# A fourth slot for expert weights, x1 read back for the last stage, and another order of the weight loads

## The reference

```
g_sel = argmax(x1 @ w_rg + b_rg)                 # 1 of 4 groups
top 2 of the 4 experts of that group             # weights from softmax, renormalised
h_e = silu(x1 @ w_gate[e]) * (x1 @ w_up[e])      # 1024 -> 256, 16 experts in all
y   = sum over a token's two experts of weight * (h_e @ w_down[e])
out = LN2(alpha * x1 + y)
```

## Time and profile before

| | us |
|---|---|
| median of 3 runs | 827.02 (824.53, 827.02, 830.73) |
| the profiled execution | 824.47 |
| its span, first to last instruction | 822.5 |
| TensorE busy | 740.1 (90%) |
| VectorE busy | 555.3 (68%) |
| ScalarE busy | 391.7 (48%) |
| GpSimd busy | 43.7 (5%) |
| DMA moved | 129.86 MB, mean 158 GB/s |

### The profile page before, as it was taken

How to read it: one execution, slowest core, us unless ns; L and a number is a source line. 1 busy time by engine, 2 the same in 40 slices (tenths; PEclk the granted TensorE clock), 3 DMA queues, 4 the chain that set the end, 5 groups by cost and what they waited for, 6 DMA issues and landing times.

```text
span 822.5 us, 13533 instructions
## 1 busy us (share of the span) xinstructions
PE 740.1 (90%) x5359; PEld 648.1 (79%) x5359; DVE 555.3 (68%) x1020; ACT 391.7 (48%) x651; POOL 43.7 (5%) x39
## 2 busy tenths in 40 slices
PE   6999999999999999888899999998459988899784
PEld 5989999999998999666678999998447766676531
DVE  4244966888644877998753565755648888888537
ACT  4348752558327332344555432111237877778502
POOL 0000000000000000000000000000010111010064
PEclk8999999999999999999999999999569999999977
DMA  7333122221333241332101963812427999999263
GB/s 235 103 112 101 52 70 86 66 68 26 122 108 116 66 148 53 116 129 69 67 29 42 351 232 107 299 45 83 160 77 255 378 389 386 385 387 386 68 230 115
DMA packets 92799, 129.86 MB, mean 158 GB/s; under 512 B 8576, under 2 KB 75136, under 8 KB 92736
## 3 DMA queue, kind: packets, MB, share of 16 engines
q1 hardware_dynamic: 87072, 112.21, 40.2%
q0 software_dynamic: 3360, 12.06, 4.2%
q10 hardware_dynamic: 2304, 4.72, 1.5%
HBM read 109.02 MB, written 19.81 MB: 157 GB/s over the span
## 4 chain that ended last, share of the span: by engine, by line
PE 67%; DVE 14%; issue 7%; ACT 6%; DMA 5%; SPq 1%; POOL 0%; ACTq 0%; DVEq 0%; POOLq 0%
PE pp L813 25%; PE pw L1134 12%; PE pp L1011 5%; PE pp L1157 5%; PE pp L793 3%; PE pw L871 2%; ACT w_hi L1226 2%; DVE w_lo L1672 2%; PE pp L1120 2%; DVE Lm L1861 1%; PE pw L980 1%; PE pw L1198 1%; DMA xtok<-in_x_sample_dram 1%; PE pp L769 1%; PE pw L1033 1%
## 5 line engine op out<-in xcount | busy, mean ns | idle before, releaser
L813 PE MATMUL pp<-x_hi,w_hi 128*128 128x288 f32 (+1 forms) x608 | 187.8, 309 | 2.6 <-DVE w_lo L1672 1.2
L813 PE MATMUL pp<-x_lo,w_hi 128*128 128x288 f32 (+1 forms) x608 | 179.6, 295 | 0.0
L813 PE MATMUL pp<-x_hi,w_lo 128*128 128x288 f32 (+1 forms) x608 | 179.4, 295 | 0.0
L813 PEld LDWEIGHTS pp<-x_hi,w_hi 128*128 128x128 f32 (+1 forms) x608 | 114.9, 189 | 10.6 <-issue 7.6
L813 PEld LDWEIGHTS pp<-x_lo,w_hi 128*128 128x128 f32 (+1 forms) x608 | 113.9, 187 | 0.2
L813 PEld LDWEIGHTS pp<-x_hi,w_lo 128*128 128x128 f32 (+1 forms) x608 | 113.7, 187 | 0.0
L1672 DVE TENSOR_TENSOR w_lo<-w_raw,w_hi 128x2048 fp32r<-128x2048 f32 (+1 forms) x30 | 67.1, 2236 | 43.7 <-ACT w_hi L1226 43.5
L2103 DVE TENSOR_TENSOR glo<-wgu,ghi 128x1024 fp32r<-128x1024 f32 x64 | 76.6, 1219 | 19.0 <-ACT ghi L1502 18.8
L1502 ACT ACTIVATE ghi<-wgu 128x1024 fp32r<-128x1024 f32 x64 | 65.7, 1052 | 22.4 <-DMA wgu<-in_w_up_dram 22.4
L1134 PE MATMUL pw<-ghi,xTh 128*112 128x512 f32 x128 | 53.2, 416 | 14.7 <-issue 12.3
L1226 ACT ACTIVATE w_hi<-w_raw 128x2048 fp32r<-128x2048 f32 (+1 forms) x30 | 56.0, 1865 | 5.7 <-ACT gring L1262 4.1
(11 more groups left out here) (327 smaller groups left out, 1662.2 us busy)
## 6 DMA issues: line engine op xcount, KB each, us to landing
w_raw<-in_w_in_dram SPq DMA_DIRECT2D x23, 1024.0 KB, 5.5
wgu<-in_w_gate_dram SPq DMA_DIRECT2D x16, 1024.0 KB, 11.3
wgu<-in_w_up_dram SPq DMA_DIRECT2D x16, 1024.0 KB, 14.5
wd<-in_w_down_dram SPq DMA_DIRECT2D x16, 1024.0 KB, 9.0
ys_d<-ysb SPq DMA_DIRECT2D x16, 448.0 KB, 11.2
gates_d<-gring ACTq DMA_DIRECT2D x16, 288.0 KB, 2.1
w_raw<-in_w_out_dram SPq DMA_DIRECT2D x4, 1024.0 KB, 6.5
gates_early<-gates_d SPq DMA_DIRECT2D x4, 576.0 KB, 4.0
```

The lines of the kernel that those rows point to most:

```text
L813: mm = pe.matmul(pp[0:wide, b, 0:HT], lw, rx, start=(k == 0 and y == 0), stop=(k == last and y == 2))
```

## The change

WS becomes 4. The fourth gate-and-up slot lies at `mixer_end`, on `xr` tiles 0 to 3, and the fourth down slot 16 KB further, on tile 4 of `xr` and on row 0 of `lnr`, which the second norm does not read. So expert 3's weights are loaded as soon as all of x1 is stored and turned, and expert 4's are the first that wait for a slot. x1 is read back from `x1_d` into `xr` at the end: tiles 0 to 3 after the last gate and up, tile 4 after the last down, and the scaling by alpha stands behind that. In SP's loop, the load of down for e-1 comes after the loads of gate and up for e and waits for down of e-5; the store in that turn is that of e-6 and comes last.

```diff
-WS = 3
+WS = 4
...
-        gate_up_at = (spare, raw_start, spare + 16384)
-        down_at = (o_start, raw_start + 16384, raw_start + 24576)
+        gate_up_at = (spare, raw_start, spare + 16384, mixer_end)
+        down_at = (o_start, raw_start + 16384, raw_start + 24576, mixer_end + 16384)
...
-        s_xr = sem("s_xr")
+        s_xr, s_xr4 = sem("s_xr"), sem("s_xr4")
...
             expert_gate_up(2)
             store_x1(NT - 1)
             expert_down(2)
+            sp.wait_ge(s_x1d, 16 * NT)
+            sp.wait_ge(s_tx, 2 * NT)
+            expert_gate_up(3)
+            expert_down(3)
...
             for e in range(WS, NX):
                 sp.wait_ge(m_gu, e - WS + 1)
                 expert_gate_up(e)
-                if e >= WS + 1:
-                    store_y(e - WS - 1)
-                sp.wait_ge(m_y, e - WS + 1)
-                expert_down(e)
-            for e in range(NX - WS - 1, NX):
+                if e > WS:
+                    sp.wait_ge(m_y, e - WS)
+                    expert_down(e - 1)
+                if e >= WS + 2:
+                    store_y(e - WS - 2)
+            sp.wait_ge(m_y, NX - WS)
+            expert_down(NX - 1)
+            for e in range(NX - WS - 2, NX - 2):
                 store_y(e)
+            sp.wait_ge(m_gu, NX)
+            sp.dma_start(xr[:, 0:4, :], x1_d[0:TP].rearrange("(i p) d -> p i d", p=P)).then_inc(s_xr, 16)
+            store_y(NX - 2)
+            store_y(NX - 1)
+            sp.wait_ge(m_y, NX)
+            sp.dma_start(xr[0:64, 4, :], x1_d[TP:T]).then_inc(s_xr4, 16)
...
-                if e < NT:
-                    if e == 0:
-                        dve.wait_ge(s_x1d, 16 * NT)
-                    dve.tensor_scalar(xr[:, e, :], xr[:, e, :], ALPHA, None, ALU.mult).then_inc(s_dg, 1)
             for f in range(2):
                 down_low(NX - 1, f)
             hidden_low(NX - 1)
+            for i in range(NT):
+                r = ROWS[i]
+                if i < 4:
+                    dve.wait_ge(s_xr, 112)
+                else:
+                    dve.wait_ge(s_xr4, 16)
+                dve.tensor_scalar(xr[0:r, i, :], xr[0:r, i, :], ALPHA, None, ALU.mult).then_inc(s_dg, 1)
...
                 if i == 0:
+                    dve.wait_ge(s_dg, NT)
                     dve.wait_ge(s_yg[0], 32)
```

## The result

The changed kernel takes 829.44 us (median of 20 runs, 827.15 to 837.33) against 827.25 us for the kernel before (20 runs, 823.67 to 830.73): a ratio of 1.0032, 95% interval 1.0016 to 1.0048. By the ratio that is 2.6 us more, by the medians 2.2. A second series gave 1.0021 [1.0001, 1.0041]. The forecast was 825.5 us, a gain of 1.5: the sign was wrong. The median still lies inside the stated range, 816.5 to 830, but outside the forecast's own part of it, 822 to 828.5.

What follows compares the result with a forecast made beforehand. DMA was taken to bound the expert stage: a loss of 7.7 to 10.1 us in place of 10.4, tail 0, gain taken as 1.5 us, giving 825.5 us from the median 827.02; range 816.5 to 830.

Steps and rivals of the forecast that it cites:

- the forecast's own part: Whole kernel: 0.3 to 2.7 us gained, 822 to 828.5 us with the runs' spread, chance 0.62.
- the saturated turn: SP's queue in the expert stage: with engines saturated, one expert's loads and store take 10.5 us per turn.
- the tail: After the last experts: x1 reload and scaling delay the residuals 1.3 us, hidden under the gathered-rows wait; net 0.
- The fifth tile's load: Tail: 256 KB of x1 read back after the last store, taking about 3 us alone.
- rival B: Tail reload makes results 6.2 us late, 831.7 us; sign: PE waits over 5 us for scaling; chance 0.09.
- A: Expert stage: only weights were awaited, stores hold nobody up; all experts run at 9.5 us, 816.6 us; chance 0.17.
- the price of the turn that holds y(0): SP's queue, turn of e=6: takes 12.6 us as before, y(0) lands at 647.7, in time by 1.3 us.
- the 7.7 forecast: Expert stage: y(9), the last store behind loads, lands at 742.2, needed at 734.5, 7.7 us late.
- a slow first turn: SP's queue: if the first turn stays at 12.9 us for 10.5, y(9) is 10.1 us late.
- The loss of 10.4 us: Expert stage before: gu(5) to gu(15) took 114.9 us where the free pace of 9.5 us needs 104.5.
- Rival C: Expert stage: slow first turn and slightly longer turns give back the early weights' lead; 827 to 829 us, chance 0.12.

Runs made afterwards that it cites:

- the second trace: Profile from repeating the changed kernel unedited, an execution of 830.23 us; that series measured 828.17 us, 1.0021 of the kernel before.
- the first trace: First profile of the changed kernel, an execution of 834.53 us; the median of its 20 runs was 829.44 us.
- experiment 6: Changed kernel with the store of y(e-5) in place of y(e-6) in the turn of e, and a third result buffer: 813.48 us, 0.9824 of the kernel before.
- experiment 4: Changed kernel with a third result buffer, queue order untouched: 819.88 us, 0.9909 of the kernel before.
- experiment 5: Kernel before, three slots and old queue order, with only x1 read back and scaled at the end: 826.55 us, 0.9988.
- experiment 2: Changed kernel with the old queue order, store of y(e-5) ahead of the down load, four slots and reload kept: 824.44 us, 0.9971 of the kernel before.
- experiment 9: Changed kernel with the store of y(e-6) moved in front of the down load of its turn: 828.04 us, 1.0017 of the kernel before.

## Why the prediction was wrong

**What held.** The mechanism: DMA bound before; expert 3's weights loaded in the idle stretch with no cost that a row shows; the result copy waiting for y(k) up to y(9), in place of the casts (though from expert 2 on and for 1.9 us on average, where 0.4 to 1 us from expert 3 or 4 on were forecast); the saturated turn (10.5 us forecast, 10.6 in the second trace from y(0) at 655.0 to y(9) at 750.5; 11.1 in the first); the tail hidden. The fifth tile's load took 4.0 us after issue (3 forecast), the residuals began 1.9 us later (1.3 forecast), and the next wait took it. The 2.6 us that the prediction worked out for this load from the Trainium skill's fit ("DMA: Bandwidth & Descriptors", Anatomy of one DMA) rest on a fit for DMAs that GpSimd issues; this load, issued by SP, took 4.0. The sign named for rival B was met, a wait of TensorE for the scaling over 5 us (6.2 in both traces), and B was still not true: 4.3 us of idle time stood in the same place before. The sign ought to have been the growth of that wait, or the start of the results' products. Rivals A and B are out: A's condition, that the stores hold nobody up, is what experiment 6 brings about, and there A's price of about 10.4 us is paid in full and more.

**The step that failed** is the price of the turn that holds y(0): "so the turn takes the same 12.6 us: y(0) lands at 647.7, in time by 1.3 us". The 12.6 us were read from a turn that began on an empty queue, down(3) at 629.12. The turn of y(0) in the changed kernel begins on a full one. Issues at 629.98 (up 5), 633.11 (down 4), 639.49 (up 6), 642.62 (down 5) and 643.43 (y 0) of the second trace:

```profile
wgu<-in_w_up_dram SPq DMA_DIRECT2D x1, 1024.0 KB, 10.5
wd<-in_w_down_dram SPq DMA_DIRECT2D x1, 1024.0 KB, 9.8
...
wgu<-in_w_up_dram SPq DMA_DIRECT2D x1, 1024.0 KB, 11.0
wd<-in_w_down_dram SPq DMA_DIRECT2D x1, 1024.0 KB, 11.2
ys_d<-ysb SPq DMA_DIRECT2D x1, 448.0 KB, 11.6
```

The turn began at 639.08. By then the turn of expert 5 was still in the queue: its up landed at 640.5, its down at 643.0. So y(0) landed at 655.0, 16.0 us after its turn's start and not 12.6; in the first trace and in experiment 4 it was 15.8. Its copy waited 2.4 us where 1.3 us were to be spare. The turn is 3.4 us dearer; 10.6 in place of 10.5 over nine turns adds 1; with the 7.7 forecast it makes 12.1, and 12.5 were measured for the copy of expert 11.

The trace of the kernel before held the right price. There y(0) stood in the first full turn, but in the changed kernel it stands in the second, behind the loads of 5 that go out when gu(1) ends. The second full turn of before begins with

```profile
638.65 0.37 SPq L667 DMA_DIRECT2D wd<-in_w_down_dram  x1
```

and its store, y(1), landed at 654.6: 15.9 us. I had allowed 2.4 us for "a slow first turn" without saying what makes it slow. The backlog of the turn ahead is the likely reason, but not all of it: the 12.6 us were a low reading too. In experiment 5, with the old order, the first full turn began on as empty a queue at 631.86, and its y(0), issued at 633.77, took

```profile
ys_d<-ysb SPq DMA_DIRECT2D x1, 448.0 KB, 13.8
```

which makes 15.7 us; experiment 2 has 16.1. How the 3.4 us divide between backlog and the spread between executions stays open, and by experiment 9 the first turn alone does not settle the total.

**A second omission** is the baseline. The loss of 10.4 us was read from one execution; the stage of before in experiment 5 lost 12.0. Set against each other in kind, 12.5 against 12.0, the stage changes by 0.5 us. The spans of these two executions differ by 2.2 us, and 1.2 of them stand ahead of gu(0) (609.9 against 608.7). So where the 1.7 to 2.6 us of the result are lost is not shown; what is shown is that the stage gives no gain. The first profile's 18.7 us (gu(3) to gu(15)) are no measure of the median.

**A third, small term** I did not foresee. In the first profile three of the gate-and-up products after long waits run 1.5 us longer: chain of waits, and the stretch with the granted clock as the third number from the end:

```profile
674.57 7.34 PE pw L1148 x24
...
719.20 7.33 PE pw L1148 x24
...
762.59 7.36 PE pw L1148 x24
...
773.69 5.80 PE pw L1148 x24
```

```profile
667.00:677.00 10.00, 7.57 (x35) 5.41 (x34) 9.27 (x10) 9.14 (x12) 1.30 (x1) 0.90 1.06 384
```

Ahead of the first of them TensorE had stood for 1.8 us, and it was busy for 7.9 of the 10 us from 657 on; the mean of 0.90 over the stretch is a part at 1.2 GHz among 2.4 GHz. The same wait of 1.8 us ahead of gu(5) in this trace was followed by a product of 5.8 us (granted clock 1.00 from 657 to 667 us). The second trace shows the longer product once (7.12 us), experiment 6 not after gu(1). No run tried it by itself, and how much of it the stage pays is not shown, but behind the last of the three, where no copy waits any more, gu(15) starts 11.1 us after gu(14) in place of 9.5.

Rival C named the outcome best: no gain, since a late first turn gives back the lead. Its price came partly from slower turns: the first trace has them (11.1 us), the second, nearer the median, does not (10.6).

## What to carry to other kernels

When loads are moved forward in an in-order DMA queue, look at the small transfers that fall behind them, and who waits for their landing: a store that frees a buffer needs its place or its queue more than a weight load with a slot in hand. More slots allow a deeper backlog in that queue, so look whether the buffers that it frees should grow with them: here a third result buffer was worth as much (7.5 us) as the earlier store (7.7). And the price of a turn is to be read from the turn that stands in the same place, at the same backlog, and from more than one execution: the first one on an empty queue took 12.6 us once and 15.7 us in another execution.

## What the runs showed of the hardware that I had not expected

With the engines equally full (share 1.06), a 448 KB store took 11.2 us at the median behind loads in SP's queue (9.8 in the changed kernel) and 6.6 us on ScalarE's own queue. The turn of the same 4.06 MB is not the same in every trace: from y(0) to y(9) it took 10.8 us in the profiled execution before, 10.6 and 11.1 in the two traces of the changed kernel and 11.1 in experiment 6 (y(0) at 642.2 to y(9) at 742.1), so a balance to within half a microsecond an expert can't be struck from one trace.
